# Order of casts, low halves, norms and transposes at three down projections' ends and at the first up projection's head, and one weight load moved ahead of seven other loads

## The reference

```python
def rmsnorm(x, w):
    y = xf * lax.rsqrt(jnp.mean(xf * xf, axis=-1, keepdims=True) + EPS)
    return (y * w.astype(jnp.float32)).astype(x.dtype)
...
        mix = jnp.concatenate([att, ssd, gdn], axis=-1) @ w_out[l]
        x = x + rmsnorm(mix, post_mix_norm[l])
        h = rmsnorm(x, pre_ffn_norm[l])
        f = (jax.nn.silu(h @ ffn_w_gate[l]) * (h @ ffn_w_up[l])) @ ffn_w_down[l]
        x = x + rmsnorm(f, post_ffn_norm[l])
...
def layer_norm(x, g, b=None):
    mu = jnp.mean(xf, axis=-1, keepdims=True)
    xc = xf - mu
    var = jnp.mean(xc * xc, axis=-1, keepdims=True)
    y = xc * lax.rsqrt(var + LN_EPS) * g.astype(jnp.float32)
...
def conv_ffn(x, w_up, conv_w, w_down):
    h = causal_dwconv_2(x @ w_up, conv_w)
    g, v = jnp.split(h, 2, axis=-1)
    return (jax.nn.silu(g) * v) @ w_down
...
    for layer in range(DEPTH_2):
        m = even_mixer(...) if layer % 2 == 0 else odd_mixer(...)
        x = layer_norm(ALPHA * x + m, ln_g[layer, 0], ln_b[layer, 0])
        f = conv_ffn(x, ffn_w_up[layer], ffn_conv_w[layer], ffn_w_down[layer])
        x = layer_norm(ALPHA * x + f, ln_g[layer, 1], ln_b[layer, 1])
```

## Time and profile before

| what | value |
|---|---|
| median of three runs | 1833.24 us |
| the profiled execution's own time | 1835.51 us |
| its span, first to last instruction | 1833.5 us |
| PE busy | 1789.2 us, 98% of the span |
| DVE, ACT, POOL busy | 63%, 44%, 36% |
| chain of waits that ended last | PE 90%, DVE 5%, ACT 2%, POOL 1%, DMA 1% |
| mean granted TensorE clock | 0.994 |

### The profile page before, as it was taken

The page is one execution under the profiler, slowest core; times in us unless marked ns, Lnnn a source line. Parts: engine busy times, 40 slices in busy tenths (PEclk is TensorE's granted clock), DMA queues, the critical chain, the costliest instruction groups (busy, mean ns, idle before and its releaser), DMA issues.

```text
span 1833.5 us, 23408 instructions
## 1 busy us (share of the span) xinstructions
PE 1789.2 (98%) x9552; PEld 1494.0 (81%) x9552; DVE 1155.7 (63%) x1588; ACT 805.3 (44%) x1280; POOL 662.0 (36%) x412
## 2 busy tenths in 40 slices
PE   7999988999999989999999999999999999999998
PEld 7788977888888878777788888878788898888886
DVE  5686644223348854786455766699765367776898
ACT  6665344222226643556724433366333244333562
POOL 1444433333543114311034445553200434455531
PEclk9999999999999999999999999999999999999999
DMA  5211032654656533111014555665422345555753
GB/s 202 74 58 71 8 116 71 218 202 163 229 184 247 183 122 116 47 47 47 24 71 176 204 193 187 210 246 200 127 92 92 115 142 202 184 183 190 260 202 112
DMA packets 52358, 266.68 MB, mean 145 GB/s; under 512 B 5346, under 2 KB 8458, under 8 KB 29850
## 3 DMA queue, kind: packets, MB, share of 16 engines
q1 hardware_dynamic: 52252, 265.20, 40.8%
HBM read 228.43 MB, written 38.29 MB: 145 GB/s over the span
## 4 chain that ended last, share of the span: by engine, by line
PE 90%; DVE 5%; ACT 2%; POOL 1%; DMA 1%; issue 0%; SPq 0%; ACTq 0%; DVEq 0%
PE ps L671 25%; PE ps L672 25%; PE ps L673 25%; PE ps L1280 2%; PE ps L666 1%; PE ps L668 1%; PE ps L667 1%; PE ps L1247 1%; PE ps L1243 1%; PE ps L1265 1%; POOL wL L2915 1%; PE ps L751 1%; PE ps L880 1%; ACT wH L1527 1%; DVE wL L2050 1%; PE ps L1211 1%
## 5 line engine op out<-in xcount | busy, mean ns | idle before, releaser
L671 PE MATMUL ps<-hH,wH 128*128 128x512 f32 (+1 forms) x1568 | 596.5, 380 | 5.9 <-POOL wL L2915 3.9
L673 PE MATMUL ps<-hH,wL 128*128 128x512 f32 (+1 forms) x1568 | 591.3, 377 | 0.0
L672 PE MATMUL ps<-hL,wH 128*128 128x512 f32 (+1 forms) x1568 | 591.2, 377 | 0.0
L2915 POOL TENSOR_TENSOR wL<-raw,wH 128x1024 fp32r<-128x1024 f32 (+2 forms) x82 | 196.0, 2412 | 519.7 <-ACT wH L1527 511.9
L671 PEld LDWEIGHTS ps<-hH,wH 128*128 128x128 f32 x1568 | 296.3, 189 | 61.4 <-issue 3.8
L673 PEld LDWEIGHTS ps<-hH,wL 128*128 128x128 f32 x1568 | 296.2, 189 | 54.5
L672 PEld LDWEIGHTS ps<-hL,wH 128*128 128x128 f32 x1568 | 296.5, 189 | 51.9
L1527 ACT ACTIVATE wH<-raw 128x1024 fp32r<-128x1024 f32 (+2 forms) x226 | 223.9, 1040 | 156.9 <-PE ps L673 138.9
L2139 DVE TENSOR_TENSOR wL<-raw,wH 128x1024 fp32r<-128x1024 f32 (+1 forms) x144 | 230.5, 1639 | 47.8 <-ACT wH L1527 47.8
L2715 DVE SCALAR_TENSOR_TENSOR ft<-ps,cols,ft 128x511 f32<-128x511 f32 (+1 forms) x176 | 131.6, 748 | 148.1 <-ACT ft L1955 145.0
L1955 ACT ACTIVATE ft<-ps,cols 128x512 f32<-128x512 f32 x88 | 60.6, 689 | 182.1 <-PE ps L673 182.1
(11 more groups left out here) (415 smaller groups left out, 2959.0 us busy)
## 6 DMA issues: line engine op xcount, KB each, us to landing
raw<-in_wbig SPq DMA_DIRECT2D x115, 1024.0 KB, 5.5
extra<-in_wbig SPq DMA_DIRECT2D x42, 1024.0 KB, 4.8
w_sums<-extra SPq DMA_DIRECT2D x33, 1024.0 KB, 8.6
raw<-w_sums SPq DMA_DIRECT2D x21, 768.0 KB, 6.2
extra<-w_sums SPq DMA_DIRECT2D x15, 768.0 KB, 6.3
rows<-in_rows SPq DMA_DIRECT2D x12, 512.0 KB, 7.4
raw<-in_wbig SPq DMA_DIRECT2D x18, 256.0 KB, 4.8
x<-in_x SPq DMA_DIRECT2D x8, 512.0 KB, 5.2
```

Source lines behind the costliest of these rows:

```text
L671: e.matmul(o, hi, m_hi, start=first, stop=False)
L672: e.matmul(o, hi, m_lo, start=False, stop=False)
L673: return e.matmul(o, lo, m_hi, start=False, stop=end)
L2915: e.tensor_tensor(wL[r][:, cs], raw[r][:, cs], wH[r][:, cs].bitcast(F32), ALU.subtract).then_inc(*low_pool.one(c, h))
```

## The change

**Head of the first up projection.** The transposes of `xn` tile 1 move ahead of the last three matmuls of the output projection (`inside`). On ACT and DVE `last_turn` takes tile 3's norm before tile 2's turn.

**All three downs, PE.** For j = 0, `P2` and `P3` take views 13 to 15 first and view 16 last.

**Down 0.** ACT and DVE finish tile 0 before they cast and split chunk 51, and split all of 51 before tile 1's adds. SP issues the load of chunk 53 as soon as 51's low halves are made, ahead of the wait for `even_start` and the seven loads.

**Down 1.** `finish` is cut in two (`centre` and the rest), which are placed apart. DVE makes the low halves of chunk 102, which POOL made before, between tile 1's adds; ACT casts 102 before tile 1's root. PE turns tile 1 after the token tile 3 of chunk 102 instead of after token tile 2.

**Down 2.** `centre` and `finish` stand where `finish` stood.

The diff, cut where it only repeats:

```diff
-BY_POOL = {1} | set(range(3, 19)) | set(range(52, 69)) | {102} | set(range(111, 117))
+BY_POOL = {1} | set(range(3, 19)) | set(range(52, 69)) | set(range(111, 117))
...
-            def tok(chunks, tail, sH, sL, ready, banks, emptied, between={}, early={}):
+            def tok(chunks, tail, sH, sL, ready, banks, emptied, between={}, early={}, inside={}):
...
                             m = three(ps[b][:, 0:n], sH[:, k0 + k, s], sL[:, k0 + k, s], H[:, k, :], L[:, k, :],
                                       start and k == 0, stop and k == nk - 1)
+                            if k == 2 and end and (i, j) in inside:
+                                inside[i, j]()
...
@@ -826,11 +828,13 @@
...
-                    for p in ("P2", "P3"):
-                        for v in (13, 16) if j else (13, 14, 15, 16):
-                            ready_b(v)
-                            m = part_b(v, p, 0, j, False, v == 16)
-                        m.then_inc(*dn.pe.one(n, p, j))
+                    for vs in ((13, 16),) if j else ((13, 14, 15), (16,)):
+                        for p in ("P2", "P3"):
+                            for v in vs:
+                                ready_b(v)
+                                m = part_b(v, p, 0, j, False, v == 16)
+                            if vs[-1] == 16:
+                                m.then_inc(*dn.pe.one(n, p, j))
...
             run(tok([15, 16], True, hH, hL, mixed, [4, 5, 6, 7], scaled("m", 1),
-                    {(3, 0): lambda: turn_xn(0), (3, 1): lambda: turn_xn(1)}))
+                    {(3, 0): lambda: turn_xn(0)}, inside={(3, 1): lambda: turn_xn(1)}))
...
             run(tok([101, 102], True, hH, hL, of_turn(("ln", 1)), [0, 1, 2, 3], lambda i: [odd.act.at("v", i)],
-                    {(2, 0): lambda: turn_ln1(0), (2, 1): lambda: turn_ln1(1)}))
+                    {(2, 0): lambda: turn_ln1(0), (3, 1): lambda: turn_ln1(1)}))
...
                 high_b(n, 16)
                 if n < 2:
                     split_done.add(DOWN[n] + 12)
-                    high_half(DOWN[n] + 12, 0)
-                finish(0)
-                if n < 2:
-                    high_half(DOWN[n] + 12, 1)
+                if n == 0:
+                    finish(0)
+                    high_half(51, 0)
+                    high_half(51, 1)
+                elif n == 1:
+                    high_half(101, 0)
+                    finish(0)
+                    high_half(101, 1)
+                    split(102)
+                else:
+                    finish(0)
                 finish(1)
...
             def last_turn():
-                turn("xn", 2)
                 xn_square(3)
                 xn_deviation(3)
+                turn("xn", 2)
                 turn("xn", 3)
...
-            def down(n, turn_tile, add_last, finish):
+            def down(n, turn_tile, add_last, centre, finish):
...
+                centre(2)
                 finish(2)
...
+                centre(3)
...
-                for i in range(2):
-                    add_last(i, 0, "P2", 4)
-                    add_last(i, 1, "P3", 2)
-                    if n < 2 and i == 0:
-                        split_done.add(DOWN[n] + 12)
-                        low_half(DOWN[n] + 12, 0)
-                    finish(i)
-                    if n < 2 and i == 0:
-                        low_half(DOWN[n] + 12, 1)
+                add_last(0, 0, "P2", 4)
+                add_last(0, 1, "P3", 2)
+                if n == 0:
+                    split_done.add(51)
+                    finish(0)
+                    low_half(51, 0)
+                    low_half(51, 1)
+                    add_last(1, 0, "P2", 4)
+                    add_last(1, 1, "P3", 2)
+                elif n == 1:
+                    split_done.update((101, 102))
+                    low_half(101, 0)
+                    centre(0)
+                    low_half(101, 1)
+                    finish(0)
+                    add_last(1, 0, "P2", 4)
+                    low_half(102, 0)
+                    add_last(1, 1, "P3", 2)
+                    low_half(102, 1)
+                    centre(1)
+                else:
+                    centre(0)
+                    finish(0)
+                    add_last(1, 0, "P2", 4)
+                    add_last(1, 1, "P3", 2)
+                    centre(1)
+                finish(1)
...
             def last_turn():
-                turn("xn", 2)
                 xn_scale(3)
                 xn_write(3)
+                turn("xn", 2)
                 turn("xn", 3)
...
-            down(0, lambda i: turn("res", i), add_f, finish_f)
+            down(0, lambda i: turn("res", i), add_f, lambda i: None, finish_f)
...
+            def centre_ln(n):
+                def centre(i):
+                    w.wait_ge(*ln.dve.at(n, "mv", i))
+                    w.wait_ge(*D["row"].at(n, "g"))
+                    e.scalar_tensor_tensor(x[:, i, :], x[:, i, :], st[:, 48 + 2 * i:49 + 2 * i], rows[0][:, :], ALU.subtract, ALU.mult).then_inc(*ln.dve.one(n, "centred", i))
+                return centre
+
             def finish_ln(n):
                 def finish(i):
-                    mv, rs = st[:, 48 + 2 * i:50 + 2 * i], st[:, 60 + i:61 + i]
-                    w.wait_ge(*ln.dve.at(n, "mv", i))
-                    w.wait_ge(*D["row"].at(n, "g"))
-                    e.scalar_tensor_tensor(x[:, i, :], x[:, i, :], mv[:, 0:1], rows[0][:, :], ALU.subtract, ALU.mult).then_inc(*ln.dve.one())
+                    rs = st[:, 60 + i:61 + i]
                     w.wait_ge(*ln.act.at(n, "sd", i))
-                    e.reciprocal(rs, st[:, 56 + i:57 + i]).then_inc(*ln.dve.one())
-                    w.wait_ge(*ln.dve.now())
+                    e.reciprocal(rs, st[:, 56 + i:57 + i]).then_inc(*ln.dve.one(n, "rs", i))
+                    w.wait_ge(*ln.dve.at(n, "centred", i))
+                    w.wait_ge(*ln.dve.at(n, "rs", i))
                     w.wait_ge(*D["row"].at(n, "b"))
                     e.scalar_tensor_tensor(x[:, i, :], x[:, i, :], rs, rows[1][:, :], ALU.mult, ALU.add).then_inc(*ln.dve.one(n, "x", i))
                 return finish
 
-            down(1, lambda i: turn(("ln", 1), i), add_ln(1, 1), finish_ln(1))
-            run(tok_side([101, 102], True, split, lambda i: None, {(2, 0): lambda: turn(("ln", 1), 0), (2, 1): lambda: turn(("ln", 1), 1)}))
+            down(1, lambda i: turn(("ln", 1), i), add_ln(1, 1), centre_ln(1), finish_ln(1))
+            run(tok_side([101, 102], True, split, lambda i: None, {(2, 0): lambda: turn(("ln", 1), 0), (3, 1): lambda: turn(("ln", 1), 1)}))
...
-            down(2, lambda i: None, add_ln(3, 2), finish_ln(3))
+            down(2, lambda i: None, add_ln(3, 2), centre_ln(3), finish_ln(3))
...
             down(0, row_f)
+            split(C_EVEN)
 
             for p in even_start():
                 w.wait_ge(*p)
```

More of the change, by code:

```diff
@@ L1983, in v_end @@
                 e.activation(v1[:, i, :], ps[i][:, :], ACT.Gelu_apprx_tanh).then_inc(*odd.act.one("v", i))
-            run(tok_side([101, 102], True, split, v_end, {(2, 0): lambda: turn(("ln", 1), 0), (2, 1): lambda: turn(("ln", 1), 1)}))
+            run(tok_side([101, 102], True, split, v_end, {(2, 0): lambda: turn(("ln", 1), 0), (3, 1): lambda: turn(("ln", 1), 1)}))
             later = []
```

## The result

The changed kernel takes 1820.86 us (median of 4 runs, 1820.67 to 1821.32) against 1834.44 for the kernel before (4 runs, 1832.77 to 1837.09): ratio 0.9923, 95% interval 0.9911 to 0.9936, so 13.6 us less. The prediction was 1815.0; 1820.86 lies outside the forecast's own range, 1813 to 1817, and inside the whole range, which goes up to 1822. The profiled spans are 1833.5 and 1819.1, so 14.4 us less where the sum said 18.2.

The account below looks back on a forecast made before the run. PE bounds the kernel, so time is won only where it stands still or runs at the lower clock: 5.6 + 7.8 + 4.7 + 0.1 = 18.2 us, median 1833.24 to 1815.0. Own range 1813 to 1817, whole range 1811.5 to 1822.

Parts of the forecast that it names:

- rivals 1 and 3: 1: POOL's pieces precede DVE, A gives 0.7, chance 0.11. 3: chunk 53's early load fails its purpose, B gives 2.9, 0.07.
- A: Head of the first up projection: waits of 1.07 and 3.62 shrink, the low clock behind goes; 5.6 us won.
- B: End of down 0 up to chunk 53: four PE waits and the low clock behind the last go; 7.8 us won.
- C: End of down 1 and chunks 101 and 102: three PE waits and view 16's go; 4.7 us won.
- the 3.25 goes: Before chunk 53: its earlier load removes PE's wait for POOL's low piece, 3.25 us, and the low clock behind it.
- no PE wait over 0.2 us from 650 to 690: Sign for the end of down 0 up to chunk 53: no PE wait over 0.2 us remains between 650 and 690.
- the prediction's own test: Wrong if any wait over 1.5 us stands at the places changed, or waits beyond 690 grow by several us.
- cast or POOL: Before chunk 53: its load lands early, but cast or POOL are the limit; one case of rival 3, chance 0.07.
- The 0.5 for view 16: End of down 1: PE's 0.37 wait at view 16 goes, with its restart; 0.5 us won.
- The collision with `sgw`: Down 1's end, behind chunk 102's second piece: POOL's product may hold DVE up to 2.35 us; 0.3 taken off.
- D: End of down 2: DVE's norm sets the tail, not PE; 0.1 us won though PE ends 0.5 earlier.
- What follows leaves it no shorter of work: Behind chunk 53: PE shows no wait over 0.5 us from 687 to 960, so the gain is not given back later.

Follow-up runs that it names:

- the second profile of before: The kernel before, unchanged, profiled a second time: 1831.7 us, span 1829.7.
- the bank out of the way: The changed kernel with chunk 52's result in PSUM bank 2 instead of bank 0: 1818.96 us.
- without either: The changed kernel with chunks 101 and 102 on PSUM banks 2, 3, 0, 1 and `sgw` held until x of tile 1 is written: 1818.88 us.
- the head alone: The kernel before with only the edits to the head of the first up projection: 1831.87 us, ratio 0.9984.
- the kernel with the late load: The changed kernel with the load of chunk 53 put back behind the seven other loads: 1822.95 us.
- the changed kernel with the late product: The changed kernel with POOL's product `sgw` held until DVE has written x of token tile 1: 1821.32 us.
- banks: The changed kernel with chunks 101 and 102 on PSUM banks 2, 3, 0, 1 for token tiles 0 to 3: 1819.24 us.
- the kernel with B alone: The changed kernel with the head's edits and those around chunks 101 and 102 undone: 1826.86 us, ratio 0.9949.

## Why the prediction was right, and where it was short

**The number.** 1820.86 is nearest to rivals 1 and 3, which both gave 1819.9, and neither is what happened: POOL did not keep its turn in A, and B gave 6.1, not 2.9. That the whole range held is owed to the room left for them; the sum itself came out 5.9 us short. The lower end of that range, 1811.5, does not follow from its terms: 0.8 in A, 0.3 in C and 1.5 for the runs give 1812.4.

**A** went as told, and against the profile that the sum was made from its size was right too: 5.28 against 5.6. Against the second profile of before it is 2.78, so that the size came out is in part luck. One wait of 1.21 was predicted as about 1.2; the write of `xn` took 1.75 where "about 2" stood because it began at 312.12 and not at 311.9; it ended at 313.87, and the transposes came at 313.93 where 314.0 was worked out. The clock held at 1.00, as said. The split between stall and clock was off: the two profiles of before put 2.5 on the clock, not 1.9, since the slow transposes (1.97 us instead of 1.09) belong to it too; so the stalls gave 2.8, not 3.75.

**B** failed at one step, "the 3.25 goes". The load, the cast and POOL were as predicted, and earlier than needed. But my list of what chunk 53 needs had weights and low halves only, not the PSUM bank that it writes. With bank 0 taken until DVE had read chunk 52, 1.55 stayed; 11.41 - 5.28 = 6.1 came of the 7.8. With the bank out of the way, 1.79 more came, 7.9 in all. So "no PE wait over 0.2 us from 650 to 690" was wrong, and by the prediction's own test, a wait of over 1.5 us, the account of B was wrong there. The step of the rival that had "cast or POOL" as the limit was wrong as well.

**C** failed in the same way, and by the same test: the low pieces of 102 on DVE were in time, as worked out, but DVE's own queue put the add of P3 behind the first of them, and PE needed that add's bank. 1.64 of wait stayed; 3.62 came of 4.7. The 4.7 was also added up wrongly: 0.5, 0.9, 1.46 and 1.8 make 4.66, not 5.0, so that less 0.3 it should have been 4.4 and the whole sum 17.9. The 0.5 for view 16 measured 0.55. The collision with `sgw` was foreseen and sized (its row is 3.42), but in the changed kernel it lay under PE's wait and cost nothing more; without either, C gives 276.33 - 271.07 = 5.26, which is 0.6 above what the terms make. Where that 0.6 comes from is not settled.

**D** and its 0.1 are below what the traces can tell.

**Beyond the change.** "What follows leaves it no shorter of work" was nearly right: from the even mixer on nothing grew but the two waits early in downs 1 and 2, together 0.9. In the ten other profiles they are 0.84 and 1.06 for before, and between 0.79 and 1.82 in down 1 and 0.96 and 1.84 in down 2 for nine changed ones. In down 1 that is on both sides of before; in down 2 eight of nine stand at 1.46 or more. The chain there runs from POOL's sums over `extra` to SP's load of it: in the changed kernel POOL ended a sum at 1680.47 and SP's load left at 1688.65, before at 1691.00 and 1703.11; less the 14.93 us between the kernels at this place, POOL was 4.4 later and the load 0.47. Why POOL's sums fall at another point of the projection is not settled.

**From span to median.** The prediction for the profiled execution was 1817.3, and it took 1820.99: 3.7 of the 5.9 lie there. The other 2.1 come from the step to the median: the profiled run of before stood 2.27 above its median, that of the changed kernel 0.13. The first profile of before had paid 2.5 us of clock in A and 1.7 in B; its second profile paid 0 and 1.6, the head alone 2.9 behind chunk 53, and the kernel with the late load nothing. So the clock's part of the sum is an average over runs, and I had taken one run's. It may also be why 15 runs of before scatter from 1831.93 to 1836.30 and the four of the changed kernel only from 1820.67 to 1821.32: two stalls behind which the clock could fall are gone. That is argued, not shown. Stalls with a low clock behind them remain, as this one of the changed kernel at a place that the change does not touch, where the clock is 0.50 from 254.79 to 258.79:

```profile
254.79 1.11 PE L989 MATMUL ps<-ident,yall 128*128 128x128 f32 x4 [2.78 <-DVE yall L2343]
```

And the changed kernel with the late product scatters over 2.8 us in four runs. Sum of the shortfall by spans: A 0.3, B 1.7, C 1.1, the downs 0.9, D 0.1, less 0.3 at the start: 3.8 of 18.2 - 14.4.

## What to carry to other kernels

When an operand comes earlier, list everything else that its consumer waits for, the accumulator bank it writes above all, and follow each one's last reader through that reader's own queue. Waits lie one behind the other, so an edit alone can be worth nothing and two together the whole (in the executions traced: banks 0, late product 0, both 1.64). A stall's cost in clock is read from several runs, never from one.

## What the runs showed of the hardware

The same wait of 3.62 us was followed by a granted clock of 1.00 from 317 to 321 in one run of the kernel before, by 0.54, near the 1.2 GHz level, from 318.64 to 322.81 in the other, and by 0.57 from 317 to 321 in the kernel with B alone; waits of 2.65 and 3.15 us before chunk 53 were followed by 0.60 and 0.50 over 4 us, one of 3.09 by 0.61 over 4.42, one of 2.84 by 1.00. Early in a down, a wait of 1.84 was followed by 0.57 over 4 us (the late product alone), one of 1.82 by 1.00 (the load of 53 behind, from 1199.55 to 1203.55). So the length of the stall does not decide alone.

A DVE instruction on two SBUF operands and POOL's took turns by who came first: 3.03 us instead of 1.17 where POOL had begun 0.44 earlier, 1.17 where POOL came 0.31 later, and then it was DVE's next one, 3.42 instead of 1.28, that waited. The Trainium skill, "SBUF — State Buffer", section "Who interferes with whom", says that a DVE instruction with two SBUF inputs contends with a GpSimd instruction that reads SBUF, and that the one issued first keeps the other out for its whole length. These rows agree.
